# Giving the first norm's input with features on partitions, and applying its root to the products

## The reference

```
h      = x * rsqrt(mean(x*x, axis=-1) + 1e-6) * norm_in          # 512 x 1024
proj   = h @ w_in                                                # dq dk dv dgate cq ckv kr mgate g_diff g_mla
dq, dk = rope(dq), rope(dk)                                      # tables of sine and cosine by position
cq, ckv are normed again, then projected; attention 8 times (4 heads of each of 2 kinds)
merged = sigmoid(g_diff) * (o_diff @ w_proj_diff) + sigmoid(g_mla) * (o_mla @ w_proj_mla)
x      = x + merged @ w_out
mod    = silu(cond) @ mod_w + mod_b                              # 6 x 1024 values, for the second block
second block: modulated norm, Hyena filter and projections, then a convolutional FFN, and the last norm
```

## Time and profile before

| | us |
|---|---|
| median of 3 runs | 1061.99 (1061.37 to 1062.31) |
| the profiled execution | 1061.37 |
| its span | 1059.3 |
| PE busy | 1040.0 |
| DVE busy | 665.7 |
| POOL busy | 543.7 |
| ACT busy | 418.6 |

### The profile page before, as it was taken

The page is one execution under the profiler, slowest core; times in us unless marked ns, Lnnn a source line. Parts: engine busy times, 40 slices in busy tenths (PEclk is TensorE's granted clock), DMA queues, the critical chain, the costliest instruction groups (busy, mean ns, idle before and its releaser), DMA issues.

```text
span 1059.3 us, 13471 instructions
## 1 busy us (share of the span) xinstructions
PE 1040.0 (98%) x4968; PEld 856.4 (81%) x4968; DVE 665.7 (63%) x1007; ACT 418.6 (40%) x687; POOL 543.7 (51%) x401
## 2 busy tenths in 40 slices
PE   7999999999999999999999999999999999999996
PEld 5889887877877888778888888778888888888885
DVE  5663776866499765985788847386666666520503
ACT  6223547665554243644444342442323223221222
POOL 1688895999200064234444346535465545553641
PEclk9999999999999999999999999999999999999999
DMA  6446454342446922212322113303222232223222
GB/s 257 164 168 225 133 187 153 90 163 70 179 159 238 379 104 100 93 67 80 110 83 84 54 42 155 143 33 146 87 80 79 103 135 79 80 80 135 104 80 79
DMA packets 19611, 131.92 MB, mean 125 GB/s; under 512 B 3411, under 2 KB 3811, under 8 KB 13030
## 3 DMA queue, kind: packets, MB, share of 16 engines
q1 hardware_dynamic: 8784, 92.62, 23.2%
q0 software_dynamic: 6560, 27.27, 8.0%
q10 hardware_dynamic: 4214, 11.30, 2.8%
HBM read 124.90 MB, written 6.30 MB: 124 GB/s over the span
## 4 chain that ended last, share of the span: by engine, by line
PE 95%; DVE 2%; ACT 1%; DMA 1%; issue 0%; POOL 0%; SPq 0%; POOLq 0%; ACTq 0%; DVEq 0%
PE bank L505 81%; PE bank L496 7%; PE bank L511 3%; PE bank L752 1%; PE bank L746 1%; DMA x_sb<-x_in 1%; PE bank L904 1%; PE bank L741 1%; DVE arena L2178 0%; DVE arena L2181 0%; PE bank L913 0%; PE bank L753 0%; PE bank L869 0%; ACT arena L1189 0%; DVE arena L2214 0%
## 5 line engine op out<-in xcount | busy, mean ns | idle before, releaser
L1730 POOL TENSOR_TENSOR ring_parts<-ring,ring_parts 128x1024 fp32r<-128x1024 f32 x102 | 248.7, 2442 | 266.3 <-ACT ring_parts L1189 263.5
L505 PE MATMUL bank<-hT_parts,ring_parts 128*128 128x512 f32 x1344 | 339.2, 393 | 0.8 <-ACT hT_parts L1518 0.8
L1189 ACT ACTIVATE ring_parts<-ring 128x1024 fp32r<-128x1024 f32 (+2 forms) x163 | 168.6, 1043 | 383.7 <-PE bank L505 219.9
L505 PEld LDWEIGHTS bank<-hT_parts,ring_parts 128*128 128x128 f32 x1344 | 249.6, 188 | 54.7 <-ACT hT_parts L1518 2.4
L505 PE MATMUL bank<-ring_parts,hT_parts 128*128 128x512 f32 (+1 forms) x672 | 171.6, 379 | 1.0 <-POOL ring_parts L1730 0.6
L505 PE MATMUL bank<-ring_parts,arena_parts 128*128 128x512 f32 (+1 forms) x736 | 172.4, 386 | 0.0
L505 PEld LDWEIGHTS bank<-ring_parts,arena_parts 128*128 128x128 f32 x736 | 136.6, 188 | 27.9 <-DVE arena L2416 0.3
L505 PE MATMUL bank<-arena_parts,ring_parts 128*128 128x512 f32 x592 | 148.0, 391 | 0.3 <-DVE arena_parts L2285 0.3
L505 PEld LDWEIGHTS bank<-ring_parts,hT_parts 128*128 128x128 f32 x672 | 122.4, 188 | 22.8 <-POOL ring_parts L1730 1.0
L2521 DVE SCALAR_TENSOR_TENSOR arena<-bank,small,arena 128x441 f32<-128x441 f32 (+2 forms) x176 | 122.3, 695 | 24.6 <-DVE arena L2521 1.7
L505 PEld LDWEIGHTS bank<-arena_parts,ring_parts 128*128 128x128 f32 x592 | 111.0, 188 | 25.4 <-DVE arena_parts L2285 2.1
(11 more groups left out here) (223 smaller groups left out, 1100.5 us busy)
## 6 DMA issues: line engine op xcount, KB each, us to landing
ring<-weights_in SPq DMA_DIRECT2D x39, 2048.0 KB, 8.0
arena<-mod_w_in POOLq DMA_DIRECT2D x32, 512.0 KB, 4.1
arena<-mod_w_in POOLq DMA_DIRECT2D x8, 1024.0 KB, 5.5
x_sb<-x_in SPq DMA_DIRECT2D x4, 512.0 KB, 5.7
ring<-weights_in SPq DMA_DIRECT2D x4, 512.0 KB, 8.5
mod_spill<-mod_part POOLq DMA_DIRECT2D x16, 128.0 KB, 2.1
x_sb<-x_in ACTq DMA_DIRECT2D x4, 512.0 KB, 12.2
arena<-mod_spill ACTq DMA_DIRECT2D x1, 2048.0 KB, 10.6
```

The source lines that it names most:

```text
L505: ins = nc.tensor.matmul(out, l, r, start=start and n == 0, stop=stop and n == len(passes) - 1)
L1189: return nc.scalar.activation(out, in_, ACT.Copy)
L1730: return nc.gpsimd.tensor_tensor(part(low), low, part(high), ALU.subtract)
```

## The change

The host gives `x` a second time, with features on partitions (`xT_in`). SP loads it straight into `x_low`, alternating with the pieces of the first chunk (pairs of 256 KB for `k` = 0 and 1, then pairs of 512 KB); `x` by tokens is loaded later, behind all constants and ahead of chunk DK, only for the squares. `hT` is the high part of `x * norm_in`, without the root. The root goes on later: into the sine and cosine tables for dq and dk, into ACT's copies for dv, the latents, dgate and mgate, and, for the gates, whose tokens lie along a row, by a product with `rs_row` on DVE ahead of ACT's sigmoid. `rs_row` goes through DRAM. Three of DVE's 8 modulation parts are moved from the gate stage to the first projections, with 3 MB of loads on POOL's queue. The three idle products read a row of ones that DVE sets.

The core of the diff ("..." marks what is left out):

```diff
-MOD_AFTER = (9, 11, 13, 15, 16, 17, 18, 19)
+MOD_EARLY = 3
+MOD_AFTER = (10, 12, 15, 17, 19)
+SGD_AFTER = 13
# SP
-            for m in range(TT):
-                sp.dma_start(x_sb[:, m, :], x_d[m * P:(m + 1) * P, :]).then_inc(sem(f"x_in{m}"), 16)
+            for k in range(2):
+                sp.dma_start(x_low[:, k, :], xT_d[:, k * SEQ:(k + 1) * SEQ]).then_inc(sem(f"half_landed{k}"), 16)
+                sp.dma_start(piece_parts(0)[0][:, k * 512:(k + 1) * 512],
+                             stream_d[C_DQ][:, k * 512:(k + 1) * 512]).then_inc(sem(f"half_landed{k}"), 16)
+            for p in range(1, PIECES):
+                sp.dma_start(x_low[:, 2 * p:2 * p + 2, :], ...).then_inc(sem(f"first_landed{p}"), 16)
                 sp.dma_start(piece_parts(p)[0], stream_d[C_DQ][:, p * PIECE:(p + 1) * PIECE]).then_inc(sem(f"first_landed{p}"), 16)
+            sp.dma_start(small[:, KD:], small_d[:, KD:]).then_inc(sem("constants_in"), 16)
...
+            for m in range(TT):
+                sp.dma_start(x_tok[:, m, :], x_d[m * P:(m + 1) * P, :]).then_inc(sem(f"x_in{m}"), 16)
             for c in range(C_DK, C_HYO + 2):
# PE
-            (idle products, 16 turns, and 16 more turns within first_chunk)
+            pe.wait_ge(sem("dve_step"), 1)
+            for n in (512, 512, 256):
+                nc.tensor.matmul(bank[7][:, 0:n], row[:, 0:P], row[:, 0:n], start=True, stop=True)
             def first_chunk():
+                for q in range(PIECES):
+                    (for k = 2q, 2q+1: wait n1_high k+1 and the high piece; 4 products high x high)
+                    (for k = 2q, 2q+1: wait input_split k+1; 4 products low input x high weight)
+                    (wait piece_low q+1; 8 products high input x low weight)
# ACT
-            for m in range(TT):
-                wait(f"x_in{m}", 16)
-                square(x_sb[:, m, :], SS + m, "n1", m)
-            split_high(0)
-            split_high(1)
+            act.dma_start(small[:, 0:KD], small_d[:, 0:KD]).then_inc(sem("gain_in"), 16)
+            for p in range(PIECES):
+                split_high(p)
+            for m in range(TT):
+                wait(f"x_in{m}", 16)
+                square(x_tok[:, m, :], SS + m, "n1", m)
...
-                wait("gate_done", i + 1)
+                wait("gate_scaled", i + 1 + (i >= 6))
                 nc.scalar.activation(dst, bank[i % 4], ACT.Sigmoid).then_inc(sem("gate_out"), 1)
-                if i == 2:
-                    nc.scalar.activation(sgd[:, 0:4, :], sgd[:, 0:4, :], ACT.Sigmoid).then_inc(sem("sgd_ready"), 1)
+                if i == 6:
+                    wait("gate_scaled", 7)
+                    nc.scalar.activation(sgd[:, 0:4, :], sgd[:, 0:4, :], ACT.Sigmoid).then_inc(sem("gates_ready"), 1)
# POOL
+            pool.dma_start(rs_row_d.rearrange("a (m p) -> p (a m)", p=P), st(RS, TT), ...)
+            link(nc.gpsimd.memset(mod_g[:], 0.0))
+            pool.dma_start(mod_g[0:1, :, :]..., mod_b_d).then_inc(sem("mod_b_in"), 16)
             wait("lambda_sums", 1)
             load_pool(0)
             load_pool(1)
+            for j in range(MOD_EARLY):
+                load_early(j)
# DVE
+            link(V.memset(row[:, 0:SEQ], 1.0))
+            wait("gain_in", 16)
+            for p in range(PIECES):
+                for k in (2 * p, 2 * p + 1):
+                    wait(f"first_landed{p}" if p else f"half_landed{k}", 32)
+                    V.tensor_scalar(part(hT[:, k, :]), x_low[:, k, :], sm("norm_in", k), None, ALU.mult).then_inc(sem("n1_high"), 1)
+                for k in (2 * p, 2 * p + 1):
+                    V.scalar_tensor_tensor(out=part(x_low[:, k, :]), in0=x_low[:, k, :], scalar=sm("norm_in", k),
+                                           in1=part(hT[:, k, :]), op0=ALU.mult, op1=ALU.subtract).then_inc(sem("input_split"), 1)
                 split_low(p)
...
             for i in range(8):
                 rope_tile(...)
+                if i == 4:
+                    mod_chunk(0)
                 split_low(8 + i)
+            mod_chunk(1)
             for p in range(16, 24):
                 split_low(p)
+                if p == 19:
+                    mod_chunk(2)
...
+            def scale_gate(i):
+                wait("gate_done", i + 1)
+                V.tensor_tensor(bank[i % 4], bank[i % 4], rs_row, ALU.mult).then_inc(sem("gate_scaled"), 1)
             for p in range(FIRST_GATE + 6, FIRST_PD + 4):
+                if p >= FIRST_GATE + 8:
+                    scale_gate(p - FIRST_GATE - 8)
                 split_low(p)
+                if p - FIRST_GATE == SGD_AFTER:
+                    V.tensor_tensor(first_four, first_four, (rs_row, 4 times), ALU.mult).then_inc(sem("gate_scaled"), 1)
-                if p in (FIRST_GATE + 8, FIRST_GATE + 9):
-                    split_output(p - FIRST_GATE + UNITS - 10)
+                if p in (FIRST_GATE + 9, FIRST_GATE + 10):
+                    split_output(p - FIRST_GATE + UNITS - 11)
                 if p - FIRST_GATE - 7 in NET_AFTER:
                     net_layer(NET_AFTER.index(p - FIRST_GATE - 7))
                 if p - FIRST_GATE in MOD_AFTER:
-                    mod_chunk(MOD_AFTER.index(p - FIRST_GATE))
+                    mod_chunk(MOD_EARLY + MOD_AFTER.index(p - FIRST_GATE))
```

More of the change, by code:

```diff
@@ L219, in build_program @@
         cos_t, sin_t, nsin_t = (at(109 + 0.5 * i, 128) for i in range(3))
+        cos_rs, sin_rs, nsin_rs = (at(66 + 0.5 * i, 128) for i in range(3))
         probs1 = [at(54, 1280), at(59, 1280)]
@@ L577, in first_chunk @@
-            def first_chunk():
[L580 to L584, removed]
-                    for m in range(TT):
[L586 to L600, removed]
@@ new lines, in _ @@
+            pe.wait_ge(sem("dve_step"), 1)
+            for n in (512, 512, 256):
+                nc.tensor.matmul(bank[7][:, 0:n], row[:, 0:P], row[:, 0:n], start=True, stop=True)
+            def first_chunk():
+                for q in range(PIECES):
+                    low, high = piece_parts(q)
+                    for i in range(2):
+                        k = 2 * q + i
+                        pe.wait_ge(sem("n1_high"), k + 1)
+                        if k == 0:
+                            pe.wait_ge(sem("half_high"), 1)
+                        else:
+                            pe.wait_ge(sem("piece_high"), q + 1)
+                        for m in range(TT):
+                            if k == 0:
+                                take(4 + m, "rope_out", m + 1)
+                            product3(bank[4 + m], [(tok(k, m),)], [(high[:, i * 512:(i + 1) * 512],)],
+                                     start=k == 0, stop=False, terms=((0, 0),))
+                    for i in range(2):
+                        k = 2 * q + i
+                        pe.wait_ge(sem("input_split"), low_at("n1", k))
+                        for m in range(TT):
+                            tokens = slice(m * P, (m + 1) * P)
+                            product3(bank[4 + m], [(None, x_low[:, k, tokens])], [(high[:, i * 512:(i + 1) * 512], None)],
+                                     start=False, stop=False, terms=((1, 0),))
+                    pe.wait_ge(sem("piece_low"), q + 1)
+                    for m in range(TT):
+                        product3(bank[4 + m], [(tok(2 * q + i, m), None) for i in range(2)],
+                                 [(None, low[:, i * 512:(i + 1) * 512]) for i in range(2)],
+                                 start=False, stop=q == PIECES - 1, terms=((0, 1),)).then_inc(sem("in_done"), 1)
@@ L1191, in split_high @@
             def split_high(p, past=0):
+                if p == 0:
+                    for k in range(2):
+                        wait(f"half_landed{k}", 32)
+                        s = slice(k * 512, (k + 1) * 512)
+                        low, high = piece_parts(p)
+                        copy(part(high[:, s]), low[:, s]).then_inc(sem("piece_high" if k else "half_high"), 1)
+                    return
                 if p < PIECES:
-                    wait(f"first_landed{p}", 16)
+                    wait(f"first_landed{p}", 32)
                 else:
@@ L1253, in qk_out @@
                 ins.then_inc(sem("qk_out"), 1)
-            for p in range(4, 15):
+            for p in range(5, 15):
                 split_high(p)
+            wait("roots", TT)
             for i in range(8, 12):
@@ L1999, in rope_key @@
                 return V.tensor_copy(kr2[:, :, 64:128], kr2[:, :, 0:64])
+            split_low(4)
+            wait("roots", TT)
+            by_root(nsin_rs, nsin_t)
+            by_root(sin_rs, sin_t)
             wait("rope_table", 2)
-            for p in range(4, 8):
+            link(by_root(cos_rs, cos_t))
+            for p in range(5, 8):
                 split_low(p)
@@ L2145, in _ @@
             wait("gate_out", 12)
-            wait("sgd_ready", 1)
+            wait("gates_ready", 2)
             for d in range(KD):
```

140 lines of the change are left out of this document (74 added, 66 removed).

## The result

| | before | after |
|---|---|---|
| median of 13 runs each, us | 1061.97 (1061.37 to 1062.68) | 1076.04 (1065.70 to 1078.47) |
| the profiled execution | 1061.37 | 1076.04 |
| its span | 1059.3 | 1074.2 |

The ratio is 1.0117, with a 95% interval of 1.0101 to 1.0133: the change made the kernel 14 us slower by the medians (about 12.5 by the means), where 1059.0 had been forecast, 3 us less than before. Three things are to be explained: the 14 us, where the 9.4 us of the front went, and why the runs now lie 12.8 us apart where they lay 1.3 apart.

The account below looks back on a forecast made before the run. PE was taken as the bound, busy 1040.0 of 1059.3 us. -9.4 + 1.0 + 1.9 + 4.0 = -2.5 us gave 1059.4 for the median, predicted as 1059.0; 8 in 10 range 1053.0 to 1062.7.

Parts of the forecast that it names:

- PE's start: First chunk: PE starts at 5.1 to 5.2 us once the first x pieces are rounded; bounds 4.6 and 6.2.
- DK's landing: Second chunk's load, 17th in line on its queue: landed at 25.5 us, so PE can go on at 27.9.
- The front, -9.4: Start of kernel: chunk DK's start moves from 37.26 to 27.9 us, -9.4; bounds -10.2 and -7.7.
- Part 0 ahead of the rope tiles, +1.0: First early modulation part delays rope tiles 5 to 7, which free banks for PE's turns: +1.0 us (0 to 4.3).
- The price of 8.5 us for a part: DVE's cost of one early modulation part beside POOL's modulation: between 4.1 and 10.1 us, taken as 8.5.
- The latents, +1.9: POOL's later loads and early parts' lock make the latents' roots late for DVE and PE: +1.9 us (0 to 9).
- the prediction's own sign of being wrong: Wrong if the second L869 layer starts without a wait, or PE loses more at the latents than in the gate stage.
- the slower rival: Latents: 24 early instructions each hold POOL by 0.41 us, PE waits 10.8 us, 1067.4 us in all; chance 0.08.
- The gate stage, +4.0: A modulation part delays bank 3's product, ACT's sigmoid and layer 0's sine, so PE waits: +4.0 us (3.3 to 5.0).
- The walk's step to 297.4: Gate stage: DVE's angles, scale_gate(2), split and split_output end at 297.4 us, then a modulation part begins.
- nothing swallows it: Gate stage: PE stays behind by the +4.0 us, as the sine's predecessors are fixed by PE's own layer 0.
- The clock, a rival at 0.12 and +1.7: PE's clock falls in the gate stage's 4 us pause, costing +1.7 us, 1060.7 us in all; chance 0.12.

Follow-up runs that it names:

- l_two_early: g_write_28 with two early modulation parts, behind the rope tiles and at split 19, and six in the gate stage: 1055.30 us, ratio 0.9938.
- a_write_late: The kernel after with only the roots' write to DRAM moved, issued behind POOL's modulation part 17: 1068.92 us, ratio 1.0064.
- d_three: The kernel after with three moves: a_write_late's, c_gate_order's, and the latents' roots one modulation part earlier in POOL's list: 1059.63 us, ratio 0.9984.
- c_gate_order: The kernel after with the first late modulation part behind bank 3's product with the roots in DVE's list: 1067.94 us, ratio 1.0065.
- g_write_28: d_three with the roots' write issued behind POOL's part 28 in place of 17: 1057.76 us, ratio 0.9957.
- e_idle_products: The kernel after with idle products on PE ahead of four waits (chunk DK, two for the scaled latents, layer 1): 1069.08 us, ratio 1.0082.

## Why the prediction was wrong, step by step

Of the 17.4 us between the sum of -2.5 and the +14.9 of the account above, 5.6 were missing at DK (-3.8 for -9.4), 7.5 are the lower clock, for which the sum had nothing, 3.5 more than the 2.9 forecast were lost between DK and the latents, and 0.8 is scattered. The steps in order:

**PE's start: right, by another bound.** First product at 5.27, forecast 5.1 to 5.2. But it came without a wait for data, right behind the idle products, which took 4.02 us and not 3.6 at most. The "few short waits inside" were one of 2.23 us at the second feature; the chunk ends at 29.8 and not at 27.3. Even where nothing holds DK back the chunk takes 23.7 us and not 22.1 (5.53 to 29.19 in l_two_early).

**DK's landing: this step failed first.** It was a sum of units in line, 25.5 us. For the bytes the sum was 1.7 to 2.2 us short: with the write moved, ACT starts on DK at 27.23 to 27.70. It put at nothing the write of the roots, which the text even named ("a 512-element transfer of roots on the same queue"). It costs 3.7 us of waiting at DK, and then it makes POOL late as well. No row of before could price it, as there is no transfer in pieces of 4 bytes at that place; an open upper end should have stood there, and the range had no room for one. The Trainium skill, "DMA: Bandwidth & Descriptors", section "Rules for kernel authors", says that a transfer whose last dimension isn't contiguous becomes one descriptor per element, and to rearrange it so that it is. The trace agrees that this is worth doing: four contiguous elements in place of one let the write land in 2.9 us and not 9.8, and DK 3.6 us sooner.

**The front, -9.4:** -7.6 is what it gives at DK where nothing holds it (l_two_early, 29.65), -3.8 in after. The missing 1.8 has two causes that end within half a us of each other in l_two_early: DK's bytes come 1.8 us later than forecast, and the first chunk takes longer.

**Part 0 ahead of the rope tiles, +1.0:** about right in after (0.3 us at the turns, about 1 up to dk's), and inside the bounds of 0 to 4.3 everywhere: PE waited 0.2 us there in a_write_late and d_three, 1.4 in c_gate_order, 3.8 in g_write_28. The price of 8.5 us for a part was high for after: 6.98, 4.68 and 5.60.

**The latents, +1.9:** mis-sized. In the forecast's own terms, behind PE's own shift, this stage cost 5.6 us of waits and about 2 of lower clock; the first latent product came 7.3 us later than before, where the forecast had it 6.5 earlier. So the prediction's own sign of being wrong came true: PE lost more at the latents (5.6) than in the gate stage (4.0). The chain was the one described. POOL's first product came at 37.74, 2.8 us later than before and not 5 earlier; then weights kept it waiting (8.6 us after the first load against 4.0 with the spill before); less the 1.6 in hand that makes 5.8 of the 7.0 us by which the roots were later than before, and leaves about 1 for the 24 early instructions, where 2.5 had been allowed. The waits, first of before and then of after, POOL from 30 to 135 us:

```profile
POOL arena L1744 <- DMA arena<-mod_w_in: 5.8, 2, 3.2
...
POOL mod_part L1749 <- DMA mod_spill<-mod_part: 1.4, 1, 1.4
```

```profile
POOL arena L1774 <- DMA arena<-mod_w_in: 14.7, 6, 6.1
```

The roots 7.0 late, less DVE's 1.85 of slack, and 2 for the clock make 7.1 of the 7.3. So the slower rival had the right place and the wrong mechanism: POOL was late by its loads, not by the lock.

**The gate stage, +4.0:** right within 0.1 us (a wait of 4.01, the stretch 4.1 longer) and in every link: part, product, sigmoid, sine, layer 1. The walk's step to 297.4 was some 0.2 us longer than its items add up to, which is why the part starts 8.74 us behind layer 0's start and not 8.9. And "nothing swallows it" was right.

**The clock, a rival at 0.12 and +1.7:** it fell behind three pauses in the profiled execution and cost 2.6, about 2 and 2.9 us, 7.5 in all; e_idle_products gave back 7.0 by the medians and 3.7 by the ratios. The forecast had a pause of 4 us in its own sum and still put the clock's fall apart as an unlikely case. The one row on the clock spoke for it. What the Trainium skill says there, that idle gaps of this order can send the clock back, is borne out by pauses of 3.66, 3.78, 4.01, 4.58 and 6.65 us, each with a granted clock at or near 0.50 behind it. But the length of the pause doesn't decide alone. One of 3.34 us did not cost the clock (c_gate_order), and one of 2.29 us in d_three's first chunk did (granted clock 0.50 from 10 to 12 us), while 2.23 us at the same place in after did not:

```profile
9.37 1.92 PE L517 MATMUL bank<-ring_parts,hT_parts 128*128 128x512 f32 x4 [2.29 <-ACT ring_parts L1197]
```

**The spread.** Two things vary from run to run: whether a pause costs the clock, and how late weights land. Both are seen in two executions of the same front (c_gate_order and after). The runs of after itself agree: the three under 1070 us have a mean granted clock of 0.993 to 0.996, the nine over 1075 us one of 0.988 to 0.990. Why POOL's weights are late by 4 us in one run and not in another stays open.

## What to carry to other kernels

Price a transfer by its pieces as well as by its bytes, and ask what stands behind it in every queue: 2 KB in 512 pieces held back 2 MB of weights. The pause of 4 us in the gate stage cost 7 with the clock behind it, so an order of instructions that makes one has to be walked through before it is built; here the latents' and the gate stage's were each undone by moving one item by one place. When work is taken off the front, all that ran beside it (POOL's list above all) must come as much earlier, or the gain is gone at the next meeting point.

## What was not expected of the hardware

512 pieces of 4 bytes written to DRAM took 9.8 us from issue to landing and delayed another queue's landing by 3.6 us against 128 pieces of 16. Between 30 and 34 us, with 4 MB of loads issued, the core moved 42 GB/s, and 423 where the write stood elsewhere (a_write_late). DVE's modulation part, 4.1 us beside an idle POOL, took 4.7 to 9.3 in after and g_write_28 and 10.8 in c_gate_order beside POOL's products: the Trainium skill's lock ("SBUF — State Buffer", "Who interferes with whom") again, with a factor that depends on how the two lists happen to lie.
